# A modulation computed with its vectors as the stationary operand, in four 32-column tiles, at eight places

## The reference, cut to what matters

```python
# first block, for each of two layers
x = x + rms_norm(mix(rms_norm(x)))            # residual norm 0 (layer 0), 2 (layer 1)
x = x + rms_norm(mlp(rms_norm(x)))            # residual norm 1 (layer 0), 3 (layer 1)
mlp = lambda h: square(relu(h @ w1)) @ w2     # 1024 -> 4096 -> 1024

# second block, for each of two layers i
e = silu(c) @ mod_w[i] + mod_b[i]             # c, c_ctx: vectors of 1024; mod_w[i]: 1024 x 3072
shift, scale, gate = split(e, 3)              # once for c (latent tokens), once for c_ctx
u = rms_norm(h) * (1 + scale) + shift
h = h + gate * mixer(u)
```

## Time and profile before

| | us |
|---|---|
| runs of before | 4145.75, 4135.88, 4143.25 |
| median of the three | 4143.25 |
| the profiled execution, its own time | 4144.13 |
| its span, first to last instruction | 4142.5 |
| PE busy | 3833.1 (93%) |
| DVE busy | 2058.4 (50%) |
| ACT busy | 1136.8 (27%) |
| mean granted TensorE clock | 0.959 of full speed |

### The profile page before, as it was taken

One profiled execution on the slowest core, in us unless ns is written; L12 is line 12 of the kernel. 1 busy time (PEld: TensorE's weight loads), 2 busy tenths in 40 slices (PEclk: granted clock), 3 DMA queues, 4 the chain that ended last, 5 costly groups with the idle time before them and its releaser, 6 DMA issues. The chain is left out here.

```text
span 4142.5 us, 44540 instructions
## 1 busy us (share of the span) xinstructions
PE 3833.1 (93%) x16250; PEld 2479.6 (60%) x16250; DVE 2058.4 (50%) x3726; ACT 1136.8 (27%) x2079; POOL 142.6 (3%) x227
## 2 busy tenths in 40 slices
PE   6998999998889999999999999999697999999989
PEld 2445688874445888866565656565354555555554
DVE  3743453533553635446666666666303555555540
ACT  1112100011331000103343444434100444444430
POOL 6500000000000000000000000000000000000000
PEclk8998899987998999889999999999899999999999
DMA  7521323321013332421010111111011121111111
GB/s 151 138 71 46 102 76 97 82 77 48 22 46 88 90 91 72 107 77 36 26 32 29 30 30 30 30 30 31 15 51 46 48 56 56 56 56 56 56 41 53
DMA packets 456432, 246.26 MB, mean 59 GB/s; under 512 B 44256, under 2 KB 448352, under 8 KB 456320
## 3 DMA queue, kind: packets, MB, share of 16 engines
q1 hardware_dynamic: 420384, 216.15, 18.8%
q0 software_dynamic: 14144, 28.36, 2.6%
q10 hardware_dynamic: 21792, 0.22, 0.4%
HBM read 229.83 MB, written 14.80 MB: 59 GB/s over the span
## 5 line engine op out<-in xcount | busy, mean ns | idle before, releaser
L1152 PE MATMUL bank<-hT,ring 128*128 128x512 f32 (+1 forms) x1664 | 634.0, 531 | 23.4 <-DVE hT L1527 19.8
L1628 PE MATMUL bank<-hT,ring 128*128 128x512 f32 (+1 forms) x1536 | 521.1, 491 | 21.0 <-DVE big L1880 16.3
L1152 PEld LDWEIGHTS bank<-hT,ring 128*128 128x128 f32 x1664 | 310.8, 191 | 300.8 <-issue 269.5
L1628 PEld LDWEIGHTS bank<-hT,ring 128*128 128x128 f32 x1536 | 287.4, 190 | 250.3 <-issue 212.5
L326 PE MATMUL bank<-big,ring 128*128 128x512 f32 (+1 forms) x1024 | 391.9, 546 | 12.1 <-DVE big L1892 8.4
L326 PEld LDWEIGHTS bank<-big,ring 128*128 128x128 f32 x1024 | 196.7, 192 | 206.0 <-issue 185.5
L1057 ACT ACTIVATE arena<-bank 128x512 f32<-128x512 f32 (+2 forms) x224 | 118.3, 528 | 461.7 <-PE bank L1050 461.6
L456 PE MATMUL bank<-big,arena 128*128 128x256 f32 x1024 | 228.8, 379 | 0.0
L456 PEld LDWEIGHTS bank<-big,arena 128*128 128x128 f32 x1024 | 194.6, 190 | 26.5
L1025 DVE CUSTOM_DVE_ANT_0 arena<-bank,big 128x512 f32<-128x512 f32 (+2 forms) x152 | 101.3, 666 | 199.7 <-PE bank L1005 199.7
L1623 PEld LDWEIGHTS bank<-ring,hT 128*128 128x128 f32 x1536 | 177.7, 192 | 30.4 <-DVE arena L1847 17.0
(11 more groups left out here) (278 smaller groups left out, 5515.4 us busy)
## 6 DMA issues: line engine op xcount, KB each, us to landing
ring<-in_mlp_w SPq DMA_DIRECT2D x128, 512.0 KB, 5.2
ring<-in_a_w_in SPq DMA_DIRECT2D x64, 512.0 KB, 4.0
ring<-in_b_w_in SPq DMA_DIRECT2D x64, 512.0 KB, 4.0
ring<-in_mod_w SPq DMA_DIRECT2D x48, 512.0 KB, 3.7
ring<-in_even_w_in SPq DMA_DIRECT2D x32, 512.0 KB, 4.0
bias_d<-tb POOLq DMA_DIRECT2D x96, 128.0 KB, 3.4
big<-bias_d POOLq DMA_DIRECT2D x16, 768.0 KB, 5.4
ring<-in_a_w_out SPq DMA_DIRECT2D x16, 512.0 KB, 3.7
```

The costliest lines, as they stand in the source:

```text
L1152: mm = pe.matmul(bk(b + n)[0:m, 0:z - a], ring[s][:, k, 0:m], (rhs or hcol)(k, a, z), start=k == 0, stop=k == kt - 1)
L1628: mm = pe.matmul(flatb[2][:, a:z], ring[s][:, k, :], hT[:, k, a:z], start=k == 0, stop=k == KT - 1)
```

## The change

1. In `pe_mod` the operands change places. `cc` becomes [128, 8, 32] with columns 2 to 31 zero (one more memset, in `dve_mod`), and is the stationary operand, 128 x 32; the slab is the moving one, 128 x 128. Four blocks go together: block j of the four writes partitions 32j to 32j+31 of bank 5, so it sits in the j-th 32-column strip of the array. For each k the four strips follow each other.
2. The result has columns and vectors the other way round (two useful rows in each strip), so it is copied by DVE into `tb` (`dve_mod_copy`), transposed by PE (`pe_mod_turn`, one 128 x 128 transpose for four blocks) and added to the bias by DVE (`dve_mod_add`, one instruction).
3. The 48 blocks are cut differently: 8 in each residual norm, all ahead of the sums, and 4 + 4 in each MLP, at the start of PE's steps 7 (`modx`, slots 0 to 3) and 13 (`mody`, slots 4 to 7). Copies are in the same step on DVE, transposes at the start of steps 8 and 14, additions on DVE in steps 8 and 14. The eight blocks of norms 0 and 2 are transposed at the start of step 2 of the MLP behind them, those of norm 1 behind `pe_low`, those of norm 3 right behind the norm.
4. In every step of the MLP DVE makes `u2` before the sums S1 and S2 of the next step, not after them.
5. DVE's wait for POOL's bias transfers (`b_w`) stands in the copy of norm 0, not after the first weight sums of MLP 0. `dve_gsc(0)` moves from behind norm 2 to behind `dve_low`.

```diff
-                ("mod0", range(8), 1), ("mod0b", range(3), 1),
-                ("up0a", range(8), 2), ("down0a", range(8), 2), ("up0b", range(8), 2), ("down0b", range(8), 2),
+                ("mod0", range(8), 1),
+                ("up0a", range(8), 2), ("modx0", range(4), 1), ("down0a", range(8), 2), ("mody0", range(4, 8), 1),
+                ("up0b", range(8), 2), ("down0b", range(8), 2),
...
         def sp_mlp(sp, mlp):
             for st in mlp.steps:
+                if st.s - 1 in MOD_STEP:
+                    sp_mod(sp, 4 * mlp.i + MOD_STEP[st.s - 1])
...
         def pe_mlp(pe, mlp):
             for st in mlp.steps:
                 s = st.s
+                if s == 2:
+                    pe_mod_turn(pe, 4 * mlp.i)
+                if s in MOD_STEP:
+                    pe_mod(pe, 4 * mlp.i + MOD_STEP[s])
+                if s - 1 in MOD_STEP:
+                    pe_mod_turn(pe, 4 * mlp.i + MOD_STEP[s - 1])
...
+                done(P6)
+                dve.wait_ge(m_copied, mlp.past("copied") + 2 * s + 1)
+                dve.tensor_tensor(u2, p1s[e], st.X, ALU.add).then_inc(m_u2, 1)
                 if nxt:
                     weights(nxt, S1)
                     weights(nxt, S2)
                 if final and j > 0:
                     for n in range(max(1, ta - 2), ta):
                         summed(n)
-                done(P6)
-                dve.wait_ge(m_copied, mlp.past("copied") + 2 * s + 1)
-                dve.tensor_tensor(u2, p1s[e], st.X, ALU.add).then_inc(m_u2, 1)
+                if s == 2:
+                    dve_mod_add(dve, 4 * mlp.i)
+                if s in MOD_STEP:
+                    dve_mod_copy(dve, 4 * mlp.i + MOD_STEP[s])
+                if s - 1 in MOD_STEP:
+                    dve_mod_add(dve, 4 * mlp.i + MOD_STEP[s - 1])
...
         def pe_residual(pe, r, c):
-            first, last = MODS[r.i], MODS[r.i + 1]
-            pe_mod(pe, r.i, first, first + 5)
+            pe_mod(pe, (0, 3, 4, 7)[r.i])
             for k in range(KT):
                 pe.wait_ge(n_sq, r.pre.k + k + 1)
                 for j, (a, z) in enumerate(spans(c)):
                     m = pe.matmul(bk(6 + j)[:, 0:z - a], ones, sqb[:, k, a:z], start=k == 0, stop=k == KT - 1)
-                if k == KT - 1:
-                    m.then_inc(n_sum, 1)
-                elif k % 2:
-                    pe_mod(pe, r.i, first + 5 + k // 2, first + 6 + k // 2)
-            pe_mod(pe, r.i, first + 8, last)
+            m.then_inc(n_sum, 1)
...
+        MODS = [("mod0", 0, 8, 0), ("modx0", 8, 4, 0), ("mody0", 12, 4, 4), ("mod1", 16, 8, 0),
+                ("mod2", 24, 8, 0), ("modx1", 32, 4, 0), ("mody1", 36, 4, 4), ("mod3", 40, 8, 0)]
+        MOD_STEP = {7: 1, 13: 2}
...
+        def pe_mod(pe, b):
+            phase, n0, blocks, s0 = MODS[b]
+            if b == 0:
                 pe.wait_ge(md_c, 3)
+            else:
+                pe.wait_ge(md_b, b + (2 if b > 3 else 0))
+            for q in range(blocks // 4):
+                for j in range(4):
+                    arrived(pe, phase, s0 + 4 * q + j, 0)
                 for k in range(KT):
-                    mm = pe.matmul(bk(5)[:, 2 * n:2 * n + 2], ring[s][:, k, :], cc[:, k, :],
-                                   start=k == 0, stop=k == KT - 1, skip_group_check=True)
-                mm.then_inc(slab_done[s], 1)
+                    for j in range(4):
+                        mm = pe.matmul(bk(5)[32 * j:32 * j + 32, P * q:P * q + P], cc[:, k, :],
+                                       ring[s0 + 4 * q + j][:, k, :], start=k == 0, stop=k == KT - 1,
+                                       skip_group_check=True)
+                        if k == KT - 1:
+                            mm.then_inc(slab_done[s0 + 4 * q + j], 1)
+
+        def dve_mod_copy(dve, b):
+            phase, n0, blocks, s0 = MODS[b]
+            if b == 0:
+                dve.wait_ge(b_w, 16 * 8 * 12)
+            for s in range(blocks):
+                multiplied(dve, phase, s0 + s, 0)
+            dve.tensor_copy(mod_raw[:, 0:32 * blocks], bk(5)[:, 0:32 * blocks]).then_inc(md_r, 1)
+
+        def pe_mod_turn(pe, b):
+            pe.wait_ge(md_r, b + 1)
+            for q in range(MODS[b][2] // 4):
+                m = pe.transpose(bk(5)[:, C + P * q:C + P * q + P], mod_raw[:, P * q:P * q + P], ident)
+            m.then_inc(md_t, 1)
+
+        def dve_mod_add(dve, b):
+            dve.wait_ge(md_t, b + 1)
+            dve.tensor_tensor(mods[:, :, :, :].rearrange("p a n c -> p (a n) c")[:, n0:n0 + blocks, :],
...
```

More of the change, by code:

```diff
@@ L694, in dve_residual @@
                         .then_inc(r_x, 1)
+            dve_mod_copy(dve, (0, 3, 4, 7)[r.i])
             if g_pre is not None:
@@ L1430, in program @@
         mb = sb("mb", [P, 48])
-        cc, ce = (sb(x, [P, KT, 2]) for x in ("cc", "ce"))
+        cc, ce = sb("cc", [P, KT, 32]), sb("ce", [P, KT, 2])
         lamv = part(8704, 256).rearrange("p (n d) -> p n d", n=4)
         lamp = part(8960, 128).rearrange("p (n d) -> p n d", n=2)
-        md_in, md_e, md_c, md_b = (sem("mod_" + x) for x in ("in", "e", "c", "b"))
+        md_in, md_e, md_c, md_b, md_r, md_t = (sem("mod_" + x) for x in ("in", "e", "c", "b", "r", "t"))
         mod_w = [d["mod_w_2"][i].rearrange("(k p) n -> p k n", p=P) for i in range(2)]
-        MODS = [0, 11, 22, 33, 48]
+        MODS = [("mod0", 0, 8, 0), ("modx0", 8, 4, 0), ("mody0", 12, 4, 4), ("mod1", 16, 8, 0),
+                ("mod2", 24, 8, 0), ("modx1", 32, 4, 0), ("mody1", 36, 4, 4), ("mod3", 40, 8, 0)]
+        MOD_STEP = {7: 1, 13: 2}
+        mod_raw = tb[:, :, :].rearrange("p a b -> p (a b)")[:, 512:768]
         def act_mod_in(act):
@@ L1470, in dve_mod_out @@
[L1470 to L1475, removed]
-                dve.tensor_tensor(mods[:, :, :, :].rearrange("p a n c -> p (a n) c")[:, n0:n1, c],
-                                  bk(5)[:, 2 * n0:2 * n1].rearrange("p (n c) -> p n c", c=2)[:, :, c],
-                                  mb[:, n0:n1], ALU.add).then_inc(md_b, 1)
+            phase, n0, blocks, s0 = MODS[b]
@@ new lines, in sp_mod @@
+            for s in range(blocks):
+                n = n0 + s
+                load(sp, phase, s0 + s, 0, mod_w[n // 24][:, :, P * (n % 24):P * (n % 24) + P])
+        def pe_mod(pe, b):
+            phase, n0, blocks, s0 = MODS[b]
+            if b == 0:
+                pe.wait_ge(md_c, 3)
+            else:
[3 more added lines that the diff above has]
+                    arrived(pe, phase, s0 + 4 * q + j, 0)
+                for k in range(KT):
+                    for j in range(4):
[4 more added lines that the diff above has]
+                            mm.then_inc(slab_done[s0 + 4 * q + j], 1)
@@ new lines, in dve_mod_add @@
+        def dve_mod_add(dve, b):
+            phase, n0, blocks, s0 = MODS[b]
+            dve.wait_ge(md_t, b + 1)
+            dve.tensor_tensor(mods[:, :, :, :].rearrange("p a n c -> p (a n) c")[:, n0:n0 + blocks, :],
+                              bk(5)[:, C:C + 32 * blocks].rearrange("p (n x) -> p n x", x=32)[:, :, 0:2],
+                              mb[:, :].rearrange("p (n o) -> p n o", o=1)[:, n0:n0 + blocks, :]
+                              .to_broadcast([P, blocks, 2]), ALU.add).then_inc(md_b, 1)
@@ L1480, in act_mod @@
         def act_mod(act):
             act.wait_ge(md_in, 64)
-            act.activation(ce[:, :, :].rearrange("p k c -> p (k c)"), cc[:, :, :].rearrange("p k c -> p (k c)"),
-                           ACT.Exp, scale=-1.0).then_inc(md_e, 1)
+            act.activation(ce[:, :, :], cc[:, :, 0:2], ACT.Exp, scale=-1.0).then_inc(md_e, 1)
             act.wait_ge(md_c, 5)
@@ L1489, in dve_mod @@
             dve.wait_ge(md_e, 1)
-            cf, ef = (x[:, :, :].rearrange("p k c -> p (k c)") for x in (cc, ce))
+            cf, ef = cc[:, :, 0:2], ce[:, :, :]
+            dve.memset(cc[:, :, 2:32], 0.0)
             dve.tensor_scalar(ef, ef, 1.0, None, ALU.add).then_inc(md_c, 1)
@@ L2270, in _ @@
             sp_mlp(sp, mlp0)
-            sp_mod(sp, 1)
+            sp_mod(sp, 3)
             sp_low(sp)
@@ L2276, in _ @@
             sp_linear(sp, wout1)
-            sp_mod(sp, 2)
+            sp_mod(sp, 4)
             sp_mlp(sp, mlp1)
-            sp_mod(sp, 3)
+            sp_mod(sp, 7)
             sp_dif(sp)
@@ L2298, in _ @@
             pe_low(pe, res1.pre)
+            pe_mod_turn(pe, 3)
             pe_att1(pe)
@@ L2303, in _ @@
             pe_residual(pe, res3, TT)
+            pe_mod_turn(pe, 7)
             pe.wait_ge(n_out, res3.pre.k + KT)
@@ L2365, in _ @@
             dve_residual(dve, res2, 3, 5, S)
-            dve_mod_out(dve, 2)
-            dve_gsc(dve, 0, 6)
             dve_mlp(dve, mlp1)
@@ L2370, in _ @@
             dve_modulated(dve, res3.pre, 0, 0)
-            dve_mod_out(dve, 3)
+            dve_mod_add(dve, 7)
             dve_gsc(dve, 1, 10)
```

26 lines of the change are left out of this document (7 added, 19 removed).

## The result

The change takes 4067.07 us, the median of four runs (4065.58 to 4070.91), against 4143.56 us for the kernel before on the same chip. The ratio is 0.982 with a 95% interval of 0.9803 to 0.9837, a gain of 76.5 us. A second series gave 4065.58 against 4137.55, ratio 0.9824 (0.9808 to 0.9841).

The account below looks back on a forecast made before the run. PE, busy 93% of the span, was taken as the bound, with modulation delaying the residual norms' roots. Gains in norms and projections less MLP and other losses gave 54.3 us: 4144.1 to 4090, range 4070 to 4115.

Parts of the forecast that it names:

- gains of 11.3 and 12.9 us: Residual norms 0 and 2: tiled modulation finishes before the squares, sums follow squares, so the root comes 11.3 and 12.9 us earlier.
- the first: Modulation matmuls everywhere: tiles do not overlap, 0.223 us a matmul, total 4125 us; chance 0.09.
- second: Modulation matmuls everywhere: weight loads and matmuls take turns, 0.28 us a matmul, total 4147 us, no change; chance 0.03.
- last rivals: Modulation matmuls everywhere: each tiled record runs alone, 0.54 us a matmul, total 4249 us, slower; chance 0.02.
- Positions and projections: Behind norm 1's root: projections start 26.3 us earlier; with the positions transfer freed early, 28.2 us gained in all.
- The start of step 8: Each MLP: late slabs and DVE's modulation copy make PE's transpose wait 0 to 3 us; 1 taken.
- the 75: Four residual norms before the change: total gap in us before the roots, while the stage waits for modulation only.
- eight such idles ... 5.96 in all; I count 5.5: MLP steps: making `u2` before the weight sums removes PE's waits on L598, giving back 5.5 us.
- c = 0.08: Time in us of one matmul with a 32-column tile, estimated between 0.055 and 0.11; twice that at the lower clock.
- At the lower clock 64 tiled matmuls take 10.2 us: Norms 1 and 3: modulation ahead of the sums runs at the lower clock, 896.8 to 907.0 in norm 1.
- "5 us" until sums bring the clock back: Norm 1: dense sums restore the clock after 5 us, so three sums take 1.7 us and five 0.86.
- tail case: Norms 1 and 3: clock rises early, on top of cheapest tiled matmuls and no step 8 wait; total 4072 us.

## Why the prediction was right and wrong

**Right: what bounds the kernel, and norms 0 and 2.** The stages ended where the prediction said, at squares and not at modulation, and the gains of 11.3 and 12.9 us came out to a tenth. The strips overlap, so the first, second and last rivals fell; the experiment with the strips in turn is what the first would have been, and is 30 us behind the change. The Trainium skill's rule ("TensorE: Matmul & The Clock Gate", Part 3, Packing small matmuls), by which loads of tiles with the same rows take turns with matmuls, is contradicted: four loads and four matmuls of one k, all with 128 rows, take 4 x 0.058 us in the change, less than the 0.28 of a single one by the rule, and their loads start 0.007 us apart while records of the other strips are still open. Positions and projections went as said (4.9 us earlier behind the root, prediction 5.0). The start of step 8 cost PE 0.5 us in MLP 0 and 0.2 in MLP 1, within the 0 to 3 foreseen. The four gaps before the roots add up to 73.0 us, not to the 75 that the prediction gives; no term of the sum uses that figure.

Three terms failed, all in the same direction, and they make up most of the 24.2 us between 54.3 and 78.5.

**Failed: "eight such idles ... 5.96 in all; I count 5.5".** The order of `u2` gives back 10.1 us. The eight idles were those that the timeline puts between groups of PE. What the prediction left out are 0.26 us in each of 16 steps (5.60 against 5.34 in a group of 24 records), idle that the merged row hides and only the waits of the load queue show: 5.96 + 16 x 0.26 = 10.1. That is 4.6 of the 24.2.

**Failed: c = 0.08, "since the weight loads may not halve fully".** c came out at 0.054 to 0.058, the lower end of the range, with all four strips at once. The modulation costs the MLPs 10.1 - 1.1 = 9.0 us, which the experiment with twelve blocks in each norm confirms from the other side by saving 9.1. The prediction had 14.0, less 0.5 for fewer additions of DVE: 4.5 of the 24.2. From step to step, a place costs 1.97 us instead of 2.56, 2.4 less for the four; transposes and the wait at step 8 cost 1.8 instead of 3.8, 2.0 less. The 0.5 is there, but small: PE's first product of MLP 0 comes 6.90 us behind the root instead of 8.24, and then step 0 takes 1.1 us longer, with PE waiting 2.08 us for DVE's weight sums.

**Failed: "At the lower clock 64 tiled matmuls take 10.2 us" and the "5 us" until sums bring the clock back, in norms 1 and 3.** The prediction named the right cause for the clock's staying low, two moving columns, and then left it low for matmuls that have 128. Norm 1 of the change was at 0.50 from 884.9 to 888.3 only, up to its root, so its 128 records took 5.37 us and its sums followed the squares as in norm 0. Norm 3 took 4.60 us and its sums kept up too. That is 3.2 us in norm 1 and 5.4 in norm 3, against the one profiled execution of before. At the upper clock the projections also ran 1.7 us faster than counted, and the last sums ahead of the two roots 1.0. This is the tail case "with the clock up early in norms 1 and 3, 4072", which was held to be unlikely; with c = 0.055 it is what came, and less the 4.6 us of `u2` it gives 4067.

What is left are 4 us behind norm 3. The 1.5 us that were feared for a longer stretch at the lower clock did not come (20.5 us of it before and after), and of the 2.3 us gained, 0.65 lie between the root and the second block's first matmul (1796.93 - 1775.77 = 21.16 before, 1720.05 - 1699.54 = 20.51 after). The other 1.7 lie later, in code that the change does not touch. The profiled executions of the other kernels spread there by more than that (2364.4 to 2369.3 us, without the one that has the sums in a row), so it isn't read as an effect, and no run settled it.

**Where the gain is.** Widening the moving operand alone gives 41 to 44 us, the order of `u2` alone 10 of MLP time, the order of the sums alone nothing. The overlap of the strips is worth 30 us within the change. These parts don't add up exactly, since each fills time that another leaves free. But with two moving columns and no strips the same places are slower than before, by 0.7%, although they have the new order of `u2`.

## What to carry to other kernels

A matmul of two moving columns costs as much here as one of 128 (28 records in 3 us for either), and such matmuls in a row ran at half the clock, together with what followed them; make the small operand stationary, or, if that can't be done, try a wider moving one. Where small stationary operands fill a quarter of the columns, go round the four strips for each k rather than finish one strip. Before counting stalls off a timeline, compare the length of equal groups and the waits listed for the source line: a merged group can hide idle time that only the load queue shows.

## What the runs showed of the hardware that was not expected

A float32 matmul of 32 stationary and 128 moving columns costs 0.054 to 0.058 us when the four strips are visited in rotation for each k, and 0.218 when the next one is in the same strip (0.109 a record in both traces, but in the change for each strip at once). The weight loads of different strips start 0.007 us apart, so they don't wait for one another, nor for matmuls of other strips.

In norm 2 of the kernel before, the same view of stretches has PE busy for all of 8.20 us with 40 two-column records at a granted clock of 0.50:

```profile
1301.80:1310.00 8.20, 8.20 (x40) 0.50 0.44 129
```

A busy PE is thus no sign of the upper clock, and a row of busy time shows such a stretch only with the clock beside it.

A stop of 5.45 us of PE in the experiment with `u2` last was followed by four matmuls (eight records) at half speed (3.78 us for what takes 1.89), so that this stall cost more than its length.
